# Streaming encoder step: silu of the conditioning columns ahead of the other loads, five gathered rows moved behind pass two's latents and nine placed in the gap before its routing, tile 0's end cut in three parts in the dense loop

## The chip, the cores and the metric

The kernel runs on one core of one Trainium2 chip, in Bass: each engine has its own instruction stream, and the streams meet only in semaphores. The metric is the device time of one execution in microseconds, the median of several runs.

## The reference, cut to what matters

One trunk layer for two request groups that share their weights: a prompt of 512 tokens and a sample of 32 tokens with 128 cached ones, model width 2048, all in fp32.

```python
mod = silu(c) @ w_ada + b_ada                 # shift1, scale1, gate1, shift2, scale2, gate2
h = rms_norm(x) * (1 + scale1) + shift1
proj = h @ w_in                               # queries, latents, keys, values, forget logits, two gates
lat = rms_norm(ckv);  k_nope, v = lat_all @ w_ukv
o_mla = chunk-causal softmax attention;  o_fox = causal attention with forget cumsums
merged = sigmoid(g_mla) * (o_mla @ w_o_mla) + sigmoid(g_fox) * (o_fox @ w_o_fox)
x = x + gate1 * (merged @ w_out)
h2 = rms_norm(x) * (1 + scale2) + shift2
q = h2 @ w_q                                  # 8 heads; top 16 of 128 + 128 keys, then top 16 of 256 sums
a = gelu(h2 . u_tab[expert]) * softmax(score) # 128 experts of 16384 for each token
x = x + gate2 * sum(a * v_tab[expert])
y = rms_norm(x) * final_g                     # the outputs are y and the new cache entries
```

## The kernel before

**Tiles and passes.** The 544 tokens are five tiles of up to 128: tiles 0 and 1 are group 0 (pass one), tiles 2 and 3 and the 32 sample tokens are group 1 (pass two). Both passes run the same stages: `mixers` (latents, eight heads of MLA, eight of FoX), `merge`, the output projection (`add_out`), the second norm and the query scores, from which VectorE picks the experts (`route`).

**Weights.** SP streams blocks of 1 MB from `wstream` into a ring of four slots, in the order of the list `SEQ`; a block is asked for when its slot has been used (line 389). The first 32 blocks make `mod`: 24 are multiplied on TensorE (`ada_row`, four rows and then a batch of columns, `ada_cols`), eight on VectorE (`mod_block`). TensorE's rows need the silu of `cT` (lines 807 and 808), VectorE's blocks the silu of `c_rows` (lines 809 and 810). ACT issues the loads of both, of `b_ada`, of the constants and of x_t (lines 800 to 806) ahead of both activations. After them it copies each ada row out of PSUM (`copy_rows`, line 831); TensorE's column batches wait for those copies, VectorE adds the bias to each batch (`rows_out`, line 1276), and between batches it squares x (`squares`, line 1270), for which it waits for x_t.

**The expert part.** A row is 1 MB: one row of `peer_u` or `peer_v` for each of 128 tokens, gathered by POOL (`gather_row`) into a slot; there are four slots in `first`, and four more, the ring's, once the dense loop has read its last block (the wait on `a_ps`, line 1884). VectorE takes the rows in the order of the list `ORDER`: 256 dot products (tiles 0 and 1), then 258 additions for the same tiles (two of them the residual rows), then 288 additions in 36 batches for tiles 2, 3 and the sample. The first 514 are the generator `shallow`; `take(n)` takes n of them wherever VectorE's program has room: in pass two's `mixers` as `fill`, in its merge, its output projection and its routing. What is left after the routing runs in `rest`, which does other steps at given row numbers: `N_GATES` (normalise the gates, then 26 steps of the sort by expert, one every two rows), `N_VAR0` and `N_SCALE0` (tile 0's final norm), `N_LAST` and `N_NEED` (how far the dense loop must be for each batch).

**The dense loop.** For tiles 2, 3 and the sample TensorE computes the product of every expert's `u` with every token: 128 blocks in 32 trips of four, with two PSUM banks (`dense`, line 754). ACT takes the gelu of each block and stores it to DRAM (`dense_out`, line 1153), from where POOL gathers the wanted values. TensorE leaves the loop at trip 14 (`T_RANKED`) for two transposes, for which it waits for the sort (`sort_ok`, line 770), and at trip 16 (`T_LAST`) for one, for which it waits for `last_ok`. ACT leaves it at trips 7 (`T_GATES`), 9 (`T_FIN0`) and 15 (`T_STORE0`). At trip 9 it does tile 0's `finish` (line 1165): wait for the residual, squares with a sum, then wait for VectorE's variance (`finish_var`, `y_rs`), root. At trip 15 it stores tile 0's output.

**In pass two's latents** VectorE takes 14 rows, then computes the latents' norm and the forget gates (`latents`, line 1323, one row inside), then takes eight rows, then rotates the first head's query. TensorE transposes the normed latents as they come (`lat_ok`, line 499). After the second norm VectorE waits for the first query unit, clears a part of the score buffer (line 1772), waits for the first scores and routes.

Of the kernel before, what the change touches and what calls it, by code (L numbers as in the profile page):

```python
# [6 lines left out]
D, TP, TS, PAST = 2048, 512, 32, 128  # L7
# [8 lines left out]
CG = (0, 2 * P, T)  # L16
# [124 lines left out]
def rows(t):  # L141
    return P if t < QT else TS
# [12 lines left out]
def build(nc, wstream, x_t, c_t, c_rows, b_ada, g1, g2, kvg, final_g, fbias, lat_cache, kr_cache, kf_cache, vf_cache,  # L155
          logf_cache, keys, peer_u, peer_v, aug_ones, consts, outs):
    F32, U32 = mybir.dt.float32, mybir.dt.uint32
    ACT, ALU, AX = mybir.ActivationFunctionType, mybir.AluOpType, mybir.AxisListType
# [8 lines left out]
    with ExitStack() as ctx:  # L167
# [187 lines left out]
        def unit_done(key):  # L355
            return UNIT[key] + 1
# [9 lines left out]
        S_COL = QT * SLOTS  # L366
        T_GATES, T_FIN0, T_RANKED, T_STORE0, T_LAST = 7, 9, 14, 15, 16
        BATCHES = ([(r, t) for r in range(R_ALT) for t in (2, 3)] + [(r, 2) for r in range(R_ALT, TOPK)]
# [5 lines left out]
        TAIL = len(ORDER) - FB * len(BATCHES)  # L374
        N_GATES, N_VAR0, N_SCALE0, N_LAST, N_NEED = 432, 452, 470, 500, TAIL - 1
        SORT_STEPS = 26
# [419 lines left out]
        def _(act):  # L796
            def a(out, in_, fn=ACT.Copy, **kw):
                return nc.scalar.activation(out, in_, fn, **kw)  # L798

            act.dma_start(cT[:, :, :], c_t).then_inc(c_in, 16)  # L800
            act.dma_start(late[:, 0:2 * D], c_rows.to_broadcast([P, 2 * D])).then_inc(crow_in, 16)
            act.dma_start(bad[:, :], b_ada).then_inc(bada_in, 16)
            act.dma_start(cst[:, :], consts).then_inc(cst_in, 16)
            for i in range(4):
                for g in range(2):
                    act.dma_start(og[g][:, 4 * i:4 * i + 4, :], x_t[:, 4 * i:4 * i + 4, CG[g]:CG[g + 1]]).then_inc(x_in[i], 16)
            act.wait_ge(c_in, 16)
            a(cT[:, :, :], cT[:, :, :], ACT.Silu).then_inc(silu_ok, 1)
            act.wait_ge(crow_in, 16)
            a(late[:, 0:2 * D], late[:, 0:2 * D], ACT.Silu).then_inc(crow_ok, 1)  # L810

# [352 lines left out]
            dense_out(0, True)  # L1164
            def finish(n, t, y):
                m = rows(t)
                act.wait_ge(y_pre, n + 1)
                a(sq_junk[0:m, :], y[0:m, :], ACT.Square, accum_out=stat[0:m, 0, t:t + 1])
                act.drain().then_inc(y_ss, 1)
                act.wait_ge(y_rs, n + 1)  # L1170
                a(stat[0:m, 1, t:t + 1], stat[0:m, 1, t:t + 1], ACT.Sqrt).then_inc(y_rs2, 1)

            def store(n, t, y):
# [12 lines left out]
            act.wait_ge(route_ok, 2)  # L1186
            finish(0, 0, h2_acc[0])
            with act.Fori(T_FIN0, T_STORE0) as i:
                dense_out(i)
# [24 lines left out]
        def _(dve):  # L1214
# [183 lines left out]
            def mixers(g, fill):  # L1398
                fill(14)
                latents(g, fill)  # L1400
                if g == 0:
                    dve.wait_ge(crow_ok, 1)
                fill(8)
                for i in range(NH):
# [47 lines left out]
            def second_norm(g):  # L1452
                dve.drain().then_inc(sq_ok, 1)
                norm(2 + g, [(pb[4], CG[g], CG[g + 1])])
                if g == 0:
                    coefs(g2T, 4 * KC)
                scaled(1 + g, (g,))
# [283 lines left out]
            def take(n):  # L1741
                for _ in range(n):
                    next(peer)
# [23 lines left out]
            for j in range(KC):  # L1767
                add_out(1, j)
                take(2)
            second_norm(1)  # L1770
            dve.wait_ge(proj, unit_done((1, "wq", 0)))
            v.memset(routing[1].s_head[:, :, 2, :, :], 0.0)
            dve.drain().then_inc(s_clear, 1)
            route(1, take)
            take(4)
# [264 lines left out]
```

## Time and profile before

| | us |
|---|---|
| median of 3 runs | 4278.77 (4278.7 to 4281.38) |
| the profiled execution | 4321.2 |
| its span, first to last instruction | 4319.4 |
| TensorE matmul busy | 3502.0 (81%) |
| VectorE busy | 2839.2 (66%) |
| GpSimd busy | 1461.3 (34%) |
| ACT busy | 388.0 (9%) |

Times in the rows are microseconds from the start of the span, unless marked ns. PE is TensorE's matmul, PEld its weight load, DVE is VectorE, ACT is ScalarE, POOL is GpSimd, SP is SyncE; a q behind the name is that engine's queue or sequencer. L401 is line 401 of the kernel; a line can be that of a helper, so L401 stands for every matmul and L798 for every activation.

### The profile page before, as it was taken

How to read it: one execution, taken by the hardware profiler on the slowest of the kernel's cores; microseconds unless marked ns; L12 is line 12 of the kernel's file. 1: busy time of each engine (PE TensorE's matmuls, PEld its weight loads, DVE VectorE, ACT ScalarE, POOL GpSimd, SP SyncE). 2: the span in 40 equal slices, each digit the busy share in tenths (PEclk: the TensorE clock that was granted, in tenths of full speed). 3: DMA queues.
4: the chain of work that ended last, by engine and by line, in shares of the span. 5: the costliest groups of instructions: out<-in, count | busy, mean ns of one | idle time of the engine just before them, and what ended most of it. 6: DMA issues, size and time to landing. Idle time of an engine off the chain costs nothing.

```text
span 4319.4 us, 39399 instructions
## 1 busy us (share of the span) xinstructions
PE 3502.0 (81%) x14249; PEld 2505.6 (58%) x14249; DVE 2839.2 (66%) x3456; ACT 388.0 (9%) x958; POOL 1461.3 (34%) x1094
## 2 busy tenths in 40 slices
PE   7899999999989999999986989997599998970000
PEld 5465678887845546467765667775476766750000
DVE  5354432237777886776677868986875566557998
ACT  0311110000212111010000011001000000000000
POOL 0000000000024544553343413233533666656764
PEclk9999999999999999989998999999799999995555
DMA  8577555557368998999999957789899999988997
GB/s 331 193 278 275 208 197 191 194 219 287 136 242 332 389 392 351 391 366 392 419 408 416 400 221 308 294 341 420 350 407 379 384 410 409 382 316 353 396 383 320
DMA packets 251314, 1412.71 MB, mean 327 GB/s; under 512 B 35312, under 2 KB 83456, under 8 KB 86144
## 3 DMA queue, kind: packets, MB, share of 16 engines
q0 software_dynamic: 124704, 841.18, 48.3%
q1 hardware_dynamic: 68832, 501.25, 30.0%
q10 hardware_dynamic: 57632, 68.41, 4.5%
q8 instruction: 84, 1.38, 0.1%
q14 instruction: 62, 0.51, 0.0%
HBM read 1359.60 MB, written 51.16 MB: 327 GB/s over the span
## 4 chain that ended last, share of the span: by engine, by line
PE 53%; DVE 17%; DMA 13%; issue 5%; POOL 2%; another core or an unknown queue 2%; PEld 2%; DVEq 2%; ACT 1%; ACTq 1%; PEldq 1%; SPq 0%
PE pq L401 52%; DMA first<-peer_v,experts 8%; DVE pq L1693 7%; DMA first<-peer_u,experts 4%; DVE late L1693 3%; POOL first L1849 2%; PEld pq L401 2%; DMA ring<-wstream 1%; DVE first L1683 1%; PE pq L405 1%; ACT arena L798 1%; DVE arena L1466 1%; DVE arena L1473 1%; DVE arena L1467 1%
## 5 line engine op out<-in xcount | busy, mean ns | idle before, releaser
L401 PE MATMUL pq<-h_last,ring 128*128 128x288 f32 (+2 forms) x6688 | 1712.3, 415 | 169.1 <-issue 78.1
L401 PEld LDWEIGHTS pq<-h_last,ring 128*128 128x128 f32 (+2 forms) x6688 | 1262.0, 191 | 612.3 <-issue 164.0
L1849 POOL DMA_INDIRECT first<-peer_u,experts x256 | 433.3, 1693 | 1731.8 <-DVEq L1528 1243.5
L1849 POOL DMA_INDIRECT first<-peer_v,experts x464 | 628.1, 1354 | 906.7 <-DVEq L1694 789.5
L1693 DVE SCALAR_TENSOR_TENSOR late<-first,wts,late 128x2048 f32<-128x2048 f32 x254 | 597.3, 2352 | 184.8 <-DMA first<-peer_v,experts 172.1
L401 PE MATMUL pq<-first,ring 128*128 128x256 f32 (+2 forms) x3104 | 702.1, 385 | 20.0 <-issue 9.0
L1683 DVE CUSTOM_DVE_ANT_0 first<-first,late 128x2048 f32<-128x2048 f32 x256 | 582.1, 2292 | 192.1 <-DMA first<-peer_u,experts 184.3
L401 PEld LDWEIGHTS pq<-first,ring 128*128 128x128 f32 (+2 forms) x3104 | 572.9, 187 | 143.1 <-issue 43.8
L1693 DVE SCALAR_TENSOR_TENSOR pq<-first,wts,pq 128x2048 f32<-128x2048 f32 x142 | 334.5, 2356 | 103.1 <-DMA first<-peer_v,experts 86.5
L1867 POOL DMA_INDIRECT got<-dots_dram,at_dot x288 | 317.0, 1101 | 126.7 <-issue 93.1
L401 PE MATMUL pq<-arena,ring 128*128 128x256 f32 (+2 forms) x1216 | 303.4, 407 | 46.0 <-DVEq L1435 32.1
L798 ACT ACTIVATE arena<-pq 128x256 f32<-128x256 f32 (+12 forms) x419 | 157.4, 402 | 1715.3 <-PE pq L401 1429.8
L401 PEld LDWEIGHTS pq<-arena,ring 128*128 128x128 f32 x1216 | 231.6, 194 | 116.9 <-issue 60.1
L1693 DVE SCALAR_TENSOR_TENSOR arena<-first,wts,arena 128x2048 f32<-128x2048 f32 x63 | 148.2, 2352 | 109.0 <-DMA first<-peer_v,experts 105.9
L1693 DVE SCALAR_TENSOR_TENSOR pq<-ring,wts,pq 128x2048 f32<-128x2048 f32 x80 | 188.4, 2355 | 36.8 <-DMA ring<-peer_v,experts 25.7
L401 PE MATMUL pq<-arena,cst 128*32 128x512 f32 x8 | 5.1, 795 | 251.0 <-issue 251.0
L1230 DVE CUSTOM_DVE_ANT_0 late<-ring,late 128x2048 f32<-128x2048 f32 x72 | 164.8, 2289 | 65.0 <-ACT late L798 29.4
L1431 DVE TENSOR_TENSOR arena<-arena,pq 128x256 f32<-128x256 f32 (+1 forms) x32 | 14.0, 437 | 268.6 <-ACTq L1083 267.6
L401 PE MATMUL pq<-arena 128*128 128x256 f32 (+12 forms) x592 | 153.2, 384 | 19.6 <-ACT arena L798 18.7
L1232 DVE CUSTOM_DVE_ANT_0 ring<-ring,late 128x2048 f32<-128x2048 f32 x72 | 164.6, 2287 | 0.0
L401 PEld LDWEIGHTS pq<-arena,cst 128*32 128x32 f32 x8 | 1.0, 144 | 254.3 <-issue 254.3
L401 PE MATMUL pq<-ring,h_last 128*128 128x512 f32 (+1 forms) x288 | 140.5, 619 | 2.9 <-issue 2.9
(197 smaller groups left out, 2002.2 us busy)
## 6 DMA issues: line engine op xcount, KB each, us to landing
ring<-wstream SPq DMA_DIRECT2D x478, 1024.0 KB
dots_dram<-wts ACTq DMA_DIRECT2D x8, 2304.0 KB, 8.4
dots_dram<-stage ACTq DMA_DIRECT2D x128, 144.0 KB
first<-peer_v,experts POOLq DMA_INDIRECT x464
got<-dots_dram,at_dot POOLq DMA_INDIRECT x288
first<-peer_u,experts POOLq DMA_INDIRECT x256
out<-arena ACTq DMA_DIRECT2D x6, 512.0 KB, 8.2
o_last<-x_t ACTq DMA_DIRECT2D x5, 576.0 KB, 11.1
```

The lines of the kernel that those rows point to most:

```text
L401: return nc.tensor.matmul(out, lhsT, rhs, start=start, stop=stop)
L405: return nc.tensor.transpose(out, in_, ident[0:p, 0:p])
L798: return nc.scalar.activation(out, in_, fn, **kw)
L1230: v.tensor_tensor_reduce(out=g2b, in0=ring[:, sl, :], in1=crow[:, 0, :], scale=1.0, scalar=0.0, op0=ALU.mult, op1=ALU.add, accum_out=msum[ ...
L1232: v.tensor_tensor_reduce(out=ring[:, sl, :], in0=ring[:, sl, :], in1=crow[:, 1, :], scale=1.0, scalar=0.0, op0=ALU.mult, op1=ALU.add, accu ...
L1466: v.max_index(ind[q][:, 0:8], val[q][:, 0:8], src[q])
L1467: v.match_replace(rest[q], val[q][:, 0:8], src[q], -3.0e38)
L1473: v.max_index(ind[q][:, 8:16], val[q][:, 8:16], rest[q])
L1683: v.tensor_tensor_reduce(out=row, in0=row, in1=h2, scale=1.0, scalar=0.0, op0=ALU.mult, op1=ALU.add, accum_out=wts[:, col:col + 1]).then_i ...
L1693: v.scalar_tensor_tensor(acc, row, w, acc, ALU.mult, ALU.add)
L1849: g.indirect_dma_start(out=slots[slot], out_offset=None, in_=peer_u if kind == "u" else peer_v, in_offset=bass.IndirectOffsetOnAxis(ap=exp ...
L1867: g.indirect_dma_start(out=got[:, i % LAPS, e:e + 1], out_offset=None, in_=dots_dram.rearrange("e (t o) -> (e t) o", o=1), in_offset=bass. ...
```

## The change

It has four parts. ACT waits for `cT` and takes its silu right after issuing the loads of `cT` and `c_rows`; then it issues `b_ada`, the constants and the first quarter of x_t, takes the silu of `c_rows`, and issues the other three quarters. In pass two VectorE takes nine rows ahead of the latents and thirteen behind them, instead of 14 and eight (in pass one these calls take none). Behind pass two's second norm it takes three rows before the wait for the first query unit and six before the routing; the marks in `rest` are renumbered. In the dense loop ACT does tile 0's squares at trip 9, its root at trip 13 (`T_ROOT0`), in a loop of its own from there, and its store at trip 15 as before.

```diff
--- before.py
+++ after.py
@@ -364,7 +364,7 @@
         NU = len(UNIT)
         TRIPS = NK // 4
         S_COL = QT * SLOTS
-        T_GATES, T_FIN0, T_RANKED, T_STORE0, T_LAST = 7, 9, 14, 15, 16
+        T_GATES, T_FIN0, T_ROOT0, T_RANKED, T_STORE0, T_LAST = 7, 9, 13, 14, 15, 16
         BATCHES = ([(r, t) for r in range(R_ALT) for t in (2, 3)] + [(r, 2) for r in range(R_ALT, TOPK)]
                    + [(r, QT) for r in range(QS // FB)] + [(r, 3) for r in range(R_ALT, TOPK)])
         ORDER = ([("u", 0, c) for c in range(SLOTS)] + [("u", 1, c) for c in range(SLOTS)]
@@ -372,7 +372,7 @@
                  + [("v", 1, c) for c in range(SLOTS)] + [("x", 1, 0)]
                  + [("v", t, FB * r + e) for r, t in BATCHES for e in range(FB)])
         TAIL = len(ORDER) - FB * len(BATCHES)
-        N_GATES, N_VAR0, N_SCALE0, N_LAST, N_NEED = 432, 452, 470, 500, TAIL - 1
+        N_GATES, N_VAR0, N_SCALE0, N_LAST, N_NEED = 438, 458, 480, 502, TAIL - 1
         SORT_STEPS = 26
         uses = [0] * (GR + RING)
         N_WIDE = TAIL + 2 * FB * R_ALT
@@ -799,15 +799,17 @@
 
             act.dma_start(cT[:, :, :], c_t).then_inc(c_in, 16)
             act.dma_start(late[:, 0:2 * D], c_rows.to_broadcast([P, 2 * D])).then_inc(crow_in, 16)
+            act.wait_ge(c_in, 16)
+            a(cT[:, :, :], cT[:, :, :], ACT.Silu).then_inc(silu_ok, 1)
             act.dma_start(bad[:, :], b_ada).then_inc(bada_in, 16)
             act.dma_start(cst[:, :], consts).then_inc(cst_in, 16)
-            for i in range(4):
+            for g in range(2):
+                act.dma_start(og[g][:, 0:4, :], x_t[:, 0:4, CG[g]:CG[g + 1]]).then_inc(x_in[0], 16)
+            act.wait_ge(crow_in, 16)
+            a(late[:, 0:2 * D], late[:, 0:2 * D], ACT.Silu).then_inc(crow_ok, 1)
+            for i in range(1, 4):
                 for g in range(2):
                     act.dma_start(og[g][:, 4 * i:4 * i + 4, :], x_t[:, 4 * i:4 * i + 4, CG[g]:CG[g + 1]]).then_inc(x_in[i], 16)
-            act.wait_ge(c_in, 16)
-            a(cT[:, :, :], cT[:, :, :], ACT.Silu).then_inc(silu_ok, 1)
-            act.wait_ge(crow_in, 16)
-            a(late[:, 0:2 * D], late[:, 0:2 * D], ACT.Silu).then_inc(crow_ok, 1)
 
             def root(n, c0, c1):
 
@@ -1162,13 +1164,20 @@
             act.wait_ge(zero_out, 16 * NH)
             gelu(1, SLOTS, SLOTS)
             dense_out(0, True)
-            def finish(n, t, y):
+            def finish_squares(n, t, y):
                 m = rows(t)
                 act.wait_ge(y_pre, n + 1)
                 a(sq_junk[0:m, :], y[0:m, :], ACT.Square, accum_out=stat[0:m, 0, t:t + 1])
                 act.drain().then_inc(y_ss, 1)
+
+            def finish_root(n, t):
+                m = rows(t)
                 act.wait_ge(y_rs, n + 1)
                 a(stat[0:m, 1, t:t + 1], stat[0:m, 1, t:t + 1], ACT.Sqrt).then_inc(y_rs2, 1)
+
+            def finish(n, t, y):
+                finish_squares(n, t, y)
+                finish_root(n, t)
 
             def store(n, t, y):
                 act.wait_ge(y_ok, n + 1)
@@ -1184,8 +1193,11 @@
                 dense_out(i)
             act.wait_ge(rt_used, 2 * PH)
             act.wait_ge(route_ok, 2)
-            finish(0, 0, h2_acc[0])
-            with act.Fori(T_FIN0, T_STORE0) as i:
+            finish_squares(0, 0, h2_acc[0])
+            with act.Fori(T_FIN0, T_ROOT0) as i:
+                dense_out(i)
+            finish_root(0, 0)
+            with act.Fori(T_ROOT0, T_STORE0) as i:
                 dense_out(i)
             store(0, 0, h2_acc[0])
             with act.Fori(T_STORE0, TRIPS) as i:
@@ -1396,11 +1408,11 @@
                 dve.drain().then_inc(prob_ok, 1)
 
             def mixers(g, fill):
-                fill(14)
+                fill(9)
                 latents(g, fill)
                 if g == 0:
                     dve.wait_ge(crow_ok, 1)
-                fill(8)
+                fill(13)
                 for i in range(NH):
                     if g == 0:
                         for q in range(2):
@@ -1768,9 +1780,11 @@
                 add_out(1, j)
                 take(2)
             second_norm(1)
+            take(3)
             dve.wait_ge(proj, unit_done((1, "wq", 0)))
             v.memset(routing[1].s_head[:, :, 2, :, :], 0.0)
             dve.drain().then_inc(s_clear, 1)
+            take(6)
             route(1, take)
             take(4)
             ranking = sort_by_expert()
```

## Rows read from the trace of the kernel before

**Rows 1.** The page, chain of work that ended last, by engine.

```profile
PE 53%; DVE 17%; DMA 13%; issue 5%; POOL 2%; another core or an unknown queue 2%; PEld 2%; DVEq 2%; ACT 1%; ACTq 1%; PEldq 1%; SPq 0%
```

**Rows 2.** Timeline, start: from, for, engine, line, operation, out<-in, count [idle before <-releaser].

```profile
0.76 0.41 ACTq L800 DMA_DIRECT2D cT<-c_t  x1
...
4.12 11.81 ACTq L806 DMA_DIRECT2D first<-x_t  x1
...
25.77 1.28 ACT L798 ACT_TABLE_LOAD   x1 [25.77 <-issue]
...
27.35 17.71 PE L401 MATMUL pq<-ring,cT 128*2 128x128 f32 x128 [27.35 <-ACT cT L798]
...
62.81 0.17 DVE L1221 TENSOR_TENSOR mod<-pq,bad 128x8 f32<-128x8 f32 x1 [6.41 <-PE pq L401]
```

**Rows 3.** DMA issues of the whole span: tiles, count, KB each, median us to landing.

```profile
late<-c_rows ACTq DMA_DIRECT2D x1, 2048.0 KB, 12.2
...
o_last<-x_t ACTq DMA_DIRECT2D x1, 1728.0 KB, 38.0
...
cT<-c_t ACTq DMA_DIRECT2D x1, 16.0 KB, 5.2
```

**Rows 4.** Transfers of the first 60 us; a full 5 us (last columns DMA share, GB/s).

```profile
DMA packets 6552, 20.58 MB, mean 343 GB/s; under 512 B 639, under 2 KB 4735, under 8 KB 4735
...
40.00:45.00 5.00, 4.89 (x44) 3.42 (x42) 0.77 (x1) 0.27 (x1) 0.00 (x0) 1.00 1.01 421
```

**Rows 5.** Timeline at pass two's latents; last, line 1683 alone in one stretch.

```profile
1276.02 2.29 DVE L1683 CUSTOM_DVE_ANT_0 first<-first,late 128x2048 f32<-128x2048 f32 x1 [0.81 <-DMA first<-peer_u,experts]
...
1292.80 2.29 DVE L1683 CUSTOM_DVE_ANT_0 first<-first,late 128x2048 f32<-128x2048 f32 x1 [0.18 <-DMA first<-peer_u,experts]
...
1298.87 2.53 PE L405 MATMUL pq<-cst,arena 128*128 128x128 f32 x12 [17.54 <-DVE arena L1346]
...
1344.00 0.45 DVE L1317 TENSOR_TENSOR arena<-arena,cst 64x288 f32<-64x288 f32 x1 [15.40 <-ACTq L961]
...
1305.00:1329.00 24.00, 18.14 (x16) 1.00 0.84 290
```

**Rows 6.** Timeline behind pass two's second norm: POOL's last gather before it, VectorE.

```profile
2526.62 0.94 POOL L1849 DMA_INDIRECT first<-peer_v,experts  x1 [2.98 <-DVEq L1694]
...
2546.18 1.34 DVE L1772 MEMSET arena<- 128x1536 f32 x1 [8.39 <-PE pq L401]
2565.18 1.26 DVE L1463 MAX8 arena<-arena 128x8 f32<-128x128 f32 x6 [17.67 <-ACTq L1103]
```

**Rows 7.** Timeline of the dense loop at trip 9, ACT and TensorE.

```profile
3065.74 0.20 ACT L798 ACTIVATE stat<-stat 128x1 f32<-128x1 f32 x1 [73.44 <-DVEq L1703]
...
3068.03 2.29 PE L401 MATMUL pq<-h_last,ring 128*128 128x288 f32 x4 [63.32 <-ACT stage L798]
```

**Rows 8.** Line 1693 by stretch (DVE busy, count, PEclk, DMA share, GB/s); timeline.

```profile
2918.00:2988.00 70.00, 42.92 (x19) 1.00 1.02 424
...
3068.00:3152.00 84.00, 50.79 (x22) 0.98 0.99 401
...
3153.74 8.02 PE L401 MATMUL pq<-h_last,ring 128*128 128x288 f32 x32 [0.71 <-issue]
...
3181.62 0.19 DVE L1647 SCALAR_TENSOR_TENSOR at_dot<-arena,cst 128x32 uint32<-128x32 f32 x1
...
3187.36 8.02 PE L401 MATMUL pq<-h_last,ring 128*128 128x288 f32 x32 [0.71 <-issue]
...
3220.78 0.41 PE L405 MATMUL pq<-cst,arena 128*128 128x128 f32 x2 [0.49 <-issue]
```

**Rows 9.** Timeline behind the dense loop: POOL, ACT, VectorE.

```profile
3858.86 0.94 POOL L1849 DMA_INDIRECT ring<-peer_v,experts  x1 [25.86 <-PE pq L401]
...
3961.14 2.06 ACT L798 ACTIVATE o_last<-pq 128x512 f32<-128x512 f32 x4 [81.31 <-remote]
...
3965.36 0.15 DVE L1700 TENSOR_SCALAR stat<-stat 128x1 f32<-128x1 f32 x1 [24.21 <-ACTq L1169]
```

## The prediction

> **What bounds the kernel now.** I read the chain of work that ended last first: it runs through TensorE for half of the span, then through VectorE and the row gathers [rows 1]. A share over the whole span says little here, since TensorE alone ends the first two thirds and the rows the last third, so I went on stage by stage: the timeline of the start, of pass two's latents, of the gap behind pass two's second norm, of the dense loop at trip 9, and of the end.
>
> At the start TensorE stands until 27.35 us. It needs the silu of cT (16 KB, landed 5.2 us after an issue at 0.76 us) and gets it only when ACT has issued all eight loads of x_t; the third of these held ACT's queue for 11.81 us [rows 2, 3]. In pass two TensorE stands 17.54 us before the latents' transposes, because VectorE is still in the last of 14 rows taken ahead of them; later VectorE stands 15.40 us, having taken its eight rows behind them [rows 5]. Behind the second norm VectorE stands 8.39 us and, after one memset, 17.67 us more [rows 6]. In the dense loop ACT stands 73.44 us in tile 0's finish, waiting for VectorE's variance, and TensorE, with both banks full, 63.32 us [rows 7]. That chain is what sets the end: the gather of row 647 waits until the dense loop's last block is done (line 1884), and had waited 25.86 us for it [rows 9]. From there on the tail is a fixed number of rows. So the end moves with the end of the dense loop, as long as the rows reach their gate before it.
>
> The profiled execution (4321.2 us, span 4319.4) lies 1.0% above the median of the timed runs. I make the sum on its rows and take it off the median.
>
> **Columns' silu first.** It moves one wait and one activation ahead of ten issues, and the rows' silu ahead of six. The value for TensorE: cT lands at 0.76 + 5.2 = 6.0 us; the table load and the activation took 27.35 - 25.77 = 1.58 us before [rows 2], so TensorE can start between 6.3 us (table loaded during the wait) and 7.6 us; I take 7, a start 20.3 us earlier. That is the upper end. It can't all be kept, because the transfers are then late. By 60 us 20.58 MB had moved, in the 421 GB/s that a full stretch shows this takes 48.9 us, and I allow 2 us for the first transfers to get going: the same state of loads is there 60 - 51 = 9 us earlier and no more [rows 4]. The DMAs that move on ACT's queue: b_ada and the constants go out about 5 us later, still before TensorE has four rows done (17.71 us after its start); six loads of x_t go out behind the rows' silu, which waits for c_rows (12.2 us to landing) [rows 2, 3]. Queued behind these issues on ACT are the copies of the ada rows (line 840), without which TensorE stops after its fourth row. In the trace loads of x_t gave way to other traffic: 1728 KB took 38.0 us once [rows 3]; ACT may so be held issuing until about 32 us, when the fourth row's copy would come at 33 us against 45 before, which leaves 10 to 14. VectorE's second batch of columns, at 62.81 us before, is then at 49 to 55 us. If x_t lands much later than that, VectorE's squares hold the batches and only some 4 us are left. I take 11 us, with 4 and 20 as ends. From the second batch on the stage goes at TensorE's pace as before, and all that follows waits for it, so the gain goes through.
>
> On that point the Trainium skill ("DMA: Bandwidth & Descriptors", Queues, rings and completion order) says that each DMA engine goes round its queues packet by packet, a packet holding several descriptors. By that rule the two queues share about evenly and the gain would be 8 us rather than 11; the 38.0 us of 1728 KB in [rows 3] show a smaller share for x_t than even, so I keep 11.
>
> **Nine rows ahead of the latents instead of fourteen.** Row 9 ends at 1276.02 + 2.29 = 1278.3 us, row 14 at 1295.1 [rows 5]. Freed at 1278.3, VectorE then waits for ACT's rope copies; TensorE's previous work, which needs the same copies, ended at 1298.87 - 17.54 = 1281.3, so they are there at about 1281.0. From VectorE's start to the first transpose took 1298.87 - 1295.1 = 3.8 us, so the transposes come at 1284.8: 14.1 us earlier. ACT's square root and table loads come in this stretch too and may cost 1 to 4 us more: ends 10 and 14.5. The five rows go behind: thirteen instead of eight, from about 1291.4 us. Eight rows (16 instructions) lie in 24 us of that place, 3.0 us each [rows 5]; thirteen end near 1331, and the next step, 1344.00 before, is due at 1329.9. One or two us late there are hidden, since TensorE projects keys at that time. If the cover failed wholly, the price would be 5 x 3.0 = 15 us and the gain nothing. I take 14.
>
> **Nine rows in the gap.** Three go into the 8.39 us, six into the 17.67 us [rows 6]; VectorE needs 50.79 / 22 = 2.3 us for one [rows 8], 6.9 and 13.9 us. Queued behind them on VectorE are the memset that frees ACT's first query copies, and the routing. The four slots had been asked for by 2526.62, 11 us before the gap, and the other five come at 3.0 us apiece once the first is free at about 2540: the last near 2562, before 2565.18. So they cost nothing; if they came at the dense loop's 3.7 us, the routing would start 3 us late. What they give: every mark in the later rows is reached nine rows, 9 x 3.7 = 33 us, earlier relative to the dense loop. That alone moves no end, but the next part needs it.
>
> **Tile 0's end in three parts.** The squares stay at trip 9, the root goes to trip 13, the store stays at trip 15. TensorE's 63.32 us go [rows 7], since the variance (row 458) is then done some two trips before it is asked for, as the next lines give it. What is late next is trip 14, where TensorE waits for the sort (line 770). Counted without the shift of the two earlier parts: trip 9's first two blocks end at 3068.03 - 63.32 = 3004.7 [rows 7]; a trip takes 3187.36 - 3153.74 = 33.6 us [rows 8], so it starts at 2988 and trip 14 is due at 3156. The sort's 26 steps run over 50 rows, from row 440, which falls where row 431 fell before: row 413 ended at 2918, and 19 rows lie from there to 2988 [rows 8], so at about 2987. Row 458 then comes at 2987 + 18 x 3.7 = 3054, trip 13 at 3122. Rows beside the full dense loop took 70 / 19 = 3.68 us each, with sort steps between them 84 / 22 = 3.82 [rows 8], while the transfers were at 401 to 424 GB/s: 184 to 191 us, so the sort is ready at 3171 to 3178, and some 5 us less since the last rows go faster while TensorE stands. Before it was ready at 3181.8 and asked for at 3220.78, without a wait [rows 8]. So TensorE waits 10 to 22 us there anew; I take 17, with ends 0 (rows at 3.4) and 40 (rows at 4.2 in the heavy steps). Trip 16 asks for the last experts at row 502, twelve rows on, 46 us against two trips of 67: covered. Net of this part 63.3 - 17 = 46 us, ends 23 and 63. Rows then reach their gate 34 us earlier and the dense loop ends 46 us earlier, and as the rows were early by 25.86 [rows 9], they are still there first. The renumbered marks and the root's table loads (1.3 us at most, [rows 2], where ACT otherwise waits for TensorE) cost nothing.
>
> **Sum.** 11 + 14 + 46 = 71 us: 4278.8 - 71 = **4208 us**.
>
> **Rivals.** *The sort keeps what the finish gave.* If the rows are slower beside a dense loop that no longer stands, TensorE waits 40 us at trip 14 instead of 17 and the start gives only its low end: 4 + 14 + 23 = 41 us, 4238. For it: the transfers are full there [rows 8]; against: 50 rows would need 4.2 us each.
> *The wait at the end goes or moves out.* After its last loop ACT stood 81.31 us released by nothing that the profile names, and VectorE 24.21 us behind it [rows 9]. Other code ahead of that place may remove it: 4208 - 24 = 4184. Against: nothing in the change aims at it.
> *Slower.* ACT's loop is cut once more inside the dense loop. If a hold like that of 81.31 us came at a new cut, TensorE's two banks would cover two blocks, 16.8 us, and it would lose 64.5: with one hold 4272, no difference to be seen; with holds at both ends of the two new trips 4208 + 129 = 4337, slower. It decides from the second hold on. Against: no boundary of the loops at trips 7, 9 and 15 shows one; TensorE came to trip 14 with 0.49 us of idle time [rows 8].
> The Trainium skill ("Runtime: NRT & Kernel Launch", Instruction fetch mechanics) has the rule behind such a hold: a taken branch whose target is outside the two pages at hand must fetch by DMA first. No run here shows that this was the cause of the 81.31 us.
>
> **How the numbers follow.** Forecast 0.66 (own range 4188 to 4230), sort 0.12, end wait gone 0.13, one hold 0.06, two holds 0.03. The range leaves out the holds and the far ends of the bounds: 4168 to 4246. A measurement of this kernel can tell about 0.2%, 8.6 us, from no change: faster 0.92, same 0.05, slower 0.03.
>
> **What would show it.** TensorE's first matmul at 6 to 8 us and pass two's first latents 20 to 30 us earlier; TensorE's idle time before the latents' transposes under 5 us; nine rows between the second norm and the routing, which starts no later relative to it; no wait of ACT for line 1703 in the dense loop, and one of TensorE ahead of the first transposes of line 405 in it, 10 to 25 us; the dense loop's end some 70 us earlier and the rows' gate still waiting for it. The prediction is wrong if the start's gain is gone by pass one, if the wait at trip 14 is over 40 us, or if the rows come to their gate after the dense loop's end.

## The result, and the profile after

The changed kernel took 4244.72 us (4242.57 to 4246.88, four runs) against 4279.88 us: a ratio of 0.9918, interval 0.9900 to 0.9935, that is 35 us less (28 to 43). Measured once more beside its parts it had a ratio of 0.9895 (0.9873 to 0.9917), 45 us less (36 to 54). Two single executions, one of the kernel before (7604 us) and one of the finish alone (14420 us), are left out of every figure below. The forecast was 71 us less, 4208; the time lies inside the range, near its upper end. About half of the expected gain is missing.

The profiled execution took 4246.88 us, span 4244.5. That is 75 us under the profiled execution of before, twice what the timed runs give: about 40 us of the difference are a matter of that one execution of before, which the first experiment shows.

The page's chain of work that ended last, by engine, of the changed kernel (before: [rows 1]):

```profile
PE 48%; DMA 17%; DVE 17%; POOL 6%; issue 6%; DVEq 2%; PEld 2%; ACT 1%; PEldq 1%; ACTq 1%; POOLq 0%; SPq 0%
```

These shares differ too much between executions to be compared: in second profiles they are PE 52%, DMA 15%, POOL 6% for the kernel before and PE 35%, DMA 22%, POOL 11% for the changed one. Nor has the dense loop left the chain. In this execution it is followed until a block that ends at 3770.87, and then over the store of its values to POOL's gather of the dots (chain that ended last, in order of time):

```profile
3762.86 8.01 PE pq L401 x32
...
3771.47 4.20 DMA dots_dram<-stage
3775.67 2.17 POOL got L1881
```

POOL's idle time ahead of that gather is 0.30 us, as between most of its gathers: here loop and rows are level. The start in the timeline, which answers to [rows 2]:

```profile
5.97 0.23 ACT L798 ACTIVATE cT<-cT 128x32 f32<-128x32 f32 x1 [3.00 <-DMA cT<-c_t]
6.25 5.71 PE L401 MATMUL pq<-ring,cT 128*2 128x128 f32 x32 [6.25 <-ACT cT L798]
13.15 3.66 PE L401 MATMUL pq<-ring,cT 128*2 128x128 f32 x32 [1.18 <-DMA ring<-wstream]
15.70 12.56 ACTq L812 DMA_DIRECT2D o_last<-x_t  x1
20.98 8.95 PE L401 MATMUL pq<-ring,cT 128*2 128x128 f32 x64 [4.18 <-DMA ring<-wstream]
28.86 7.86 ACTq L812 DMA_DIRECT2D o_last<-x_t  x1
39.73 0.74 ACT L798 ACTIVATE mrow<-pq 2x128 f32<-2x128 f32 x4 [22.81 <-issue]
40.57 1.84 PE L401 MATMUL pq<-cst,mrow 2*128 2x2 f32 x8 [10.64 <-ACT mrow L798]
61.50 0.17 DVE L1233 TENSOR_TENSOR mod<-pq,bad 128x8 f32<-128x8 f32 x1 [8.15 <-PE pq L401]
```

TensorE begins at 6.25 us, as forecast, but then waits for weight blocks, and after its fourth row 10.64 us for ACT's copies, which stood behind two loads of x_t that held ACT 12.56 and 7.86 us. The second batch of columns comes at 61.50 instead of 62.81. The first matmul of pass one's latents comes at 142.33 instead of 145.02: 2.7 us of the forecast 11. In the six executions with the old start that matmul comes at 143.81 to 146.82, in the six with this new one at 141.39 to 143.85.

Pass two's latents, the gap, and the dense loop at trips 13 and 14 (to [rows 5 to 8]), still from the timeline:

```profile
1285.42 2.53 PE L405 MATMUL pq<-cst,arena 128*128 128x128 f32 x12 [2.90 <-DVE arena L1358]
...
2546.44 1.34 DVE L1785 MEMSET arena<- 128x1536 f32 x1 [1.19 <-PE pq L401]
...
2564.90 2.35 DVE L1705 SCALAR_TENSOR_TENSOR late<-first,wts,late 128x2048 f32<-128x2048 f32 x1 [2.88 <-DMA first<-peer_v,experts]
...
3124.82 0.20 ACT L798 ACTIVATE stat<-stat 128x1 f32<-128x1 f32 x1
...
3180.52 0.69 PE L405 MATMUL pq<-cst,arena 128*128 128x128 f32 x2 [24.48 <-DVEq L1661]
```

The wait ahead of the transposes is 2.90 us instead of 17.54; the nine rows fit into the gap; the root at trip 13 waits for nothing; TensorE waits 24.48 us at trip 14 where 17 was forecast. And yet the memset behind the second norm comes at the same time as before, 2546.44 against 2546.18.

The end, last block of the dense loop and first gather into the ring (to [rows 9]):

```profile
3779.48 8.00 PE L401 MATMUL pq<-h_last,ring 128*128 128x288 f32 x32 [0.26 <-issue]
...
3808.10 0.94 POOL L1863 DMA_INDIRECT ring<-peer_v,experts  x1 [0.30 <-issue]
```

The loop ends at 3787.5, and POOL comes to its gate 20.6 us later, without a wait. The prediction named just this as what would prove it wrong: the rows come after the loop's end.

### The profile page after: what moved, and what is told of

The parts are those of the page before. It is cut to its first block, busy times and chain, and to the rows that moved or that the text cites. A ratio compares the mean times of both kernels' runs of the same rounds, so it can differ in the third digit from the quotient of the medians.

```text
span 4244.5 us, 39396 instructions
## 1 busy us (share of the span) xinstructions
PE 3510.5 (83%) x14249; PEld 2510.1 (59%) x14249; DVE 2838.9 (67%) x3456; ACT 382.1 (9%) x954; POOL 1483.6 (35%) x1094
## 4 chain that ended last, share of the span: by engine, by line
PE 48%; DMA 17%; DVE 17%; POOL 6%; issue 6%; DVEq 2%; PEld 2%; ACT 1%; PEldq 1%; ACTq 1%; POOLq 0%; SPq 0%
PE pq L401 47%; DMA first<-peer_v,experts 10%; DMA first<-peer_u,experts 6%; DVE pq L1705 5%; POOL first L1863 4%; DVE late L1705 3%; PEld pq L401 2%; DVE first L1695 2%; POOL got L1881 2%; DMA ring<-wstream 2%; PE pq L405 1%; ACT arena L798 1%; POOL ring L1863 1%; ACTq L812 1%; DVE arena L1478 1%
## 5 line engine op out<-in xcount | busy, mean ns | idle before, releaser
L1863 POOL DMA_INDIRECT first<-peer_u,experts x256 | 419.7, 1639 | 1746.2 <-DVEq L1540 1243.4
L1863 POOL DMA_INDIRECT first<-peer_v,experts x464 | 660.7, 1424 | 843.5 <-DVEq L1706 752.2
L1242 DVE CUSTOM_DVE_ANT_0 late<-ring,late 128x2048 f32<-128x2048 f32 x72 | 164.8, 2289 | 50.7 <-DMA ring<-wstream 24.5
## 6 DMA issues: line engine op xcount, KB each, us to landing
first<-peer_u,experts POOLq DMA_INDIRECT x256, 10.1
```

What stands on the lines that cost most here:

```text
L1242: v.tensor_tensor_reduce(out=g2b, in0=ring[:, sl, :], in1=crow[:, 0, :], scale=1.0, scalar=0.0, op0=ALU.mult, op1=ALU.add, accum_out=msum[ ...
L1863: g.indirect_dma_start(out=slots[slot], out_offset=None, in_=peer_u if kind == "u" else peer_v, in_offset=bass.IndirectOffsetOnAxis(ap=exp ...
```

## The experiments

Two theories were set against each other. **R**: the rows and their transfers set the end, the dense loop's end doesn't. **D**, the prediction's own: the dense loop's end sets it.

### Before, a second time

> The kernel before, unchanged, profiled a second time. Theory (the profiled execution of before had a slow end that the timed runs don't have): its time is 4278 to 4285 us, ACT's 81 us wait behind the dense loop and VectorE's 24 us behind it are gone or under 10 us, and the rows between 3800 and 4000 us run at a transfer share near 1.00 instead of 0.79 and 0.88; the dense loop may still end near 3855 or earlier. Rival (the excess is typical of a profiled run of before): about 4320 us again, with the 81 us wait at the same place.

It took 4284.48 us, beside 4286.8 as the median of before on that chip. Timeline of that execution:

```profile
3822.78 8.00 PE L401 MATMUL pq<-h_last,ring 128*128 128x288 f32 x32 [0.26 <-issue]
...
3845.12 0.95 POOL L1849 DMA_INDIRECT ring<-peer_v,experts  x1 [0.30 <-issue]
...
3927.99 0.20 ACT L798 ACTIVATE stat<-stat 128x1 f32<-128x1 f32 x1 [73.26 <-DVEq L1703]
```

The dense loop ends at 3830.8 (3858.6 in the first execution), POOL reaches its gate 14.3 us after that and doesn't wait. The 25.86 us of [rows 9], on which the prediction hung the end, and the 81.31 us of ACT with them, belong to one execution. The copy out of PSUM that had waited 81.31 us waits 5.58 us here; the 73.26 us above are another wait, that of tile 1's `finish` for VectorE's variance. Between 3800 and 3900 and between 3900 and 4000 us the transfers' share is 0.93 and 1.02 instead of 0.79 and 0.88. The stall at trip 9 is the same (63.73 us). So already before the change the rows were late at the gate, and the theory on the excess holds.

### The parts alone

The silu alone, on before:

```diff
+            act.wait_ge(c_in, 16)
+            a(cT[:, :, :], cT[:, :, :], ACT.Silu).then_inc(silu_ok, 1)
             act.dma_start(bad[:, :], b_ada).then_inc(bada_in, 16)
...
-            act.wait_ge(c_in, 16)
-            a(cT[:, :, :], cT[:, :, :], ACT.Silu).then_inc(silu_ok, 1)
```

> Before plus the first part alone (silu of the columns first, x_t's quarters split around the silu of the rows). Theory (the start's gain is spent by x_t's loads and by the clock, and what is left is lost where the rows wait for transfers): first latents matmul 2 to 4 us earlier than 145.02, second norm's memset within 2 us of 2546, time -3 to +2 us. Rival (the start's gain goes through): -7 us or more.

Ratio 0.9998 (0.9982 to 1.0014): 1 us less, between 8 less and 6 more, as the theory had it. First latents matmul at 142.40; pass two's transposes at 1301.15, where the five executions with the old start and the old latents have 1298.9 to 1302.9.

The latents alone:

```diff
-                fill(14)
+                fill(9)
                 latents(g, fill)
...
-                fill(8)
+                fill(13)
```

> Before plus the second part alone (nine rows ahead of pass two's latents, thirteen behind). Theory (transfers bind pass two from 1300 us on, so the rows come when the transfers allow): TensorE 13 us earlier at head 1, 0 to 3 us earlier at the second norm's memset (2546), time -4 to +1 us. Rival (TensorE binds and the gain was lost to stretches of its clock at 1.2 GHz that differ from execution to execution): 8 to 13 us earlier at the memset in an execution with as many such stretches as before, time -6 to -13 us.

Ratio 0.9978 (0.9962 to 0.9995): 9 us less (2 to 16), inside the rival's band. The transposes come at 1283.40, the memset at 2529.54, some 20 us earlier than in the second execution of before. My theory, that transfers take the 13 us back, falls: they go through. Why the changed kernel showed nothing of them at its memset is answered below.

The gap alone, the finish alone, and both:

```diff
             second_norm(1)
+            take(3)
...
+            take(6)
             route(1, take)
```

```diff
-            finish(0, 0, h2_acc[0])
-            with act.Fori(T_FIN0, T_STORE0) as i:
+            finish_squares(0, 0, h2_acc[0])
+            with act.Fori(T_FIN0, T_ROOT0) as i:
+                dense_out(i)
+            finish_root(0, 0)
+            with act.Fori(T_ROOT0, T_STORE0) as i:
                 dense_out(i)
```

> Before plus the third part alone: nine rows in the gap with the renumbered marks; tile 0's finish stays whole at trip 9. Theory R (the rows and their transfers set the end; in an ordinary execution of before POOL's first gather into the ring comes 14 us after the dense loop's end): the rows come 20 to 25 us earlier, the stall of TensorE at trip 9 stays at 55 to 70 us because the variance is now asked of row 458, the dense loop's end stays, and the gate then takes effect: time -13 to -22 us. Rival D (the dense loop's end sets the end, as the prediction had it): time 0 to -5 us.

> Before plus the fourth part alone: tile 0's end in three parts, marks and gap as before. Theory R: TensorE waits 22 to 28 us at trip 14 instead of 64 at trip 9, the dense loop ends 35 to 42 us earlier, but the rows come only 5 to 13 us earlier and so does the end: time -5 to -13 us. Rival D: time -25 to -40 us.

> Before plus the third and fourth part together (nine rows in the gap with the renumbered marks, and tile 0's end in three parts); start and latents as before. Theory (the whole gain is here: 9.9 MB more moved in the gap, worth 25 us at 400 MB per ms, and 5 MB more at trip 9, worth 13 us): time -31 to -38 us, as the whole change. Rival (the early parts carry a third of the gain): -15 to -25 us.

The gap alone: ratio 0.9981 (0.9963 to 0.9998), 8 us less (1 to 16). The finish alone: 0.9978 (0.9960 to 0.9996), 9 us less (2 to 17). Both: 0.9924 (0.9895 to 0.9953), 33 us less (20 to 45), in the band of its theory. The gap's 8 us lie between its bands: R asked for 13 to 22, D for 0 to 5. The timeline of the finish alone:

```profile
3199.90 0.69 PE L405 MATMUL pq<-cst,arena 128*128 128x128 f32 x2 [36.47 <-DVEq L1659]
...
3798.58 8.00 PE L401 MATMUL pq<-h_last,ring 128*128 128x288 f32 x32 [0.26 <-issue]
...
3849.82 0.94 POOL L1859 DMA_INDIRECT ring<-peer_v,experts  x1 [0.30 <-issue]
```

This is the run that decides. The last block, begun at 3798.58, ends near 3806.6, 24 us earlier than in the second execution of before, and the first gather into the ring comes 4.7 us later than there: the loop's end moved and the rows didn't follow. D asked for 25 to 40 us less; 9 came, inside R's 5 to 13. R's marks on the way were missed, though: TensorE waits 36.47 us at trip 14 instead of 22 to 28, the loop ends 24 us earlier instead of 35 to 42, and the rows, said to come 5 to 13 us earlier, came no earlier in this execution. Where the 9 us of the time come from is therefore not shown.

All traces agree on the main point. From the first gather into the ring to the end of the span it is 436.4 to 437.8 us in thirteen of the fourteen executions (460.5 in the first of before), and in those thirteen that gather comes 4.3 to 43.2 us behind the loop's end. So the end follows that gather, and the gather doesn't wait for the loop's end. And the gap alone:

```profile
3073.84 10.57 PE L401 MATMUL pq<-h_last,ring 128*128 128x288 f32 x32 [62.37 <-ACT stage L798]
...
3295.30 0.28 DVE L1658 TENSOR_REDUCE last_f<-pq 2x16 f32<-2x128 f32 x1 [13.97 <-PE pq L405]
```

The rows run some 25 us ahead up to row 502; there VectorE wants the last experts' transpose, which TensorE, late by its stall at trip 9, does at trip 16, and stands 13.97 us; POOL, whose first gather of dots needs what VectorE computes from it, stands 31.08 us there, and 12.4 to 16.0 us in the other executions. So the gap alone is held by the stall that the finish removes; with both edits the 13.97 us are gone. Against the second execution of before the stretch from pass two's memset to the end is 11.0 us shorter with the gap, 1.1 us longer with the finish and 32.6 us shorter with both. The times alone (8 and 9 against 33) leave open, by their intervals, whether the pair gives more than the sum.

### The sort begun earlier

```diff
-        N_GATES, N_VAR0, N_SCALE0, N_LAST, N_NEED = 438, 458, 480, 502, TAIL - 1
+        N_GATES, N_VAR0, N_SCALE0, N_LAST, N_NEED = 426, 458, 480, 502, TAIL - 1
```

> The changed kernel with the sort begun at row 426 instead of 438 (one mark; every other mark as it is). Theory R (rows and transfers set the end, the dense loop's end doesn't): TensorE's wait of 24 to 27 us at trip 14 falls under 3 us, the dense loop ends 20 to 26 us earlier, and the end stays: time -4 to +4 us against the changed kernel. Rival D (the dense loop's end sets the end): 15 to 25 us below the changed kernel.

Ratio 0.9881 (0.9861 to 0.9900), against 0.9895 (0.9873 to 0.9917) for the changed kernel on another chip: 6 us less, with overlapping intervals. The wait at trip 14 is gone (6.13 us at trip 16 in its place), the loop ends at 3763.1, 24 us earlier than in the changed kernel. D's 15 to 25 us didn't come. But R's "the end stays", within 4 us, isn't met cleanly either: from the memset to the end this execution is 10 to 15 us shorter than the two of the changed kernel. What of the loop's end reaches the rows is left open at that size.

### The changed kernel again

> The changed kernel, unchanged, profiled and timed again beside its parts. Theory (the latents' 13 us are real, and in the first profile of the changed kernel they were lost to longer stretches of the clock at 1.2 GHz between 1300 and 2000 us, which differ from execution to execution): time -36 to -48 us, 5 to 12 us below the third and fourth part alone; memset behind the second norm between 2528 and 2550 us, earlier the shorter those stretches are. Rival (rows or start take the 13 us back in this kernel every time): memset at 2544 to 2549 again, time -29 to -36 us, no better than the third and fourth part alone.

45 us less (36 to 54), as the theory had it; but the memset came at 2545.02, inside both bands (2528 to 2550 and 2544 to 2549): that row decides nothing.

### The start with the copies first

```diff
-            for i in range(1, 4):
-                for g in range(2):
-                    act.dma_start(og[g][:, 4 * i:4 * i + 4, :], x_t[:, 4 * i:4 * i + 4, CG[g]:CG[g + 1]]).then_inc(x_in[i], 16)
+            load_x(1)
...
-            for i in range(4):
+            rows_trip(0)
+            load_x(2)
+            load_x(3)
+            for i in range(1, 4):
                 rows_trip(i)
```

> The changed kernel with the last two quarters of x_t issued by ACT behind its copies of the first four ada rows, instead of ahead of them. Theory (ACT, held 12.6 and 7.9 us in issues of x_t, made TensorE's columns wait 10.6 us and used up most of what the silu gave): the copies follow the fourth ada row within 2 us, TensorE's wait ahead of the first batch of columns falls under 2 us, the second batch comes at 50 to 56 us instead of 61.5, the first latents matmul at 133 to 138 us instead of 142. Rival (the transfers bind the start; VectorE's squares of x_t's late quarters hold the second batch): second batch at 59 us or later, first latents matmul at 140 us or later. Time: by the first 2 to 10 us below the changed kernel, by the rival within 3 us of it; a measurement of this kernel hardly tells these apart, the trace does.

The start of its timeline:

```profile
30.53 1.02 PE L401 MATMUL pq<-cst,mrow 2*128 2x2 f32 x8 [0.40 <-ACT mrow L798]
31.48 14.94 PE L401 MATMUL pq<-ring,cT 128*2 128x128 f32 x128
...
43.32 1.22 DVE L1292 TENSOR_TENSOR first<-first 128x1024 f32<-128x1024 f32 x1 [2.98 <-DMA o_last<-x_t]
...
55.68 0.17 DVE L1239 TENSOR_TENSOR mod<-pq,bad 128x8 f32<-128x8 f32 x1
...
57.80 12.47 PE L401 MATMUL pq<-ring,cT 128*2 128x128 f32 x87 [9.96 <-DMA ring<-wstream]
```

The hold of ACT was real: without it the wait ahead of the columns goes from 10.64 to 0.40 us, and the second batch comes at 55.68 as forecast. But the next wait takes its place: TensorE stands 9.96 us for a weight block, and the first latents matmul comes at 139.94, 2.4 us earlier than in the changed kernel, not 4 to 9. In the last run below, which has the same edit, it comes at 142.40, no earlier than in the changed kernel. The theory holds for the copies, the rival for the stage. The ratio is 0.9886 (0.9865 to 0.9906), 49 us less than before and 4 less than the changed kernel on another chip, which its interval doesn't tell from nothing.

### The hole behind the routing heads

```diff
                     dve.drain().then_inc(rt_used, 1)
+                    fill(3)
...
-                    fill(7)
+                    fill(4)
```

> The changed kernel with the seven rows behind each routing head of pass two split: three behind the head's first selection, four at its end. VectorE idled 28.5 us for the gathers behind the heads, while the transfers stood at a share of 0.77. Theory R (filling a hole of the transfers brings the rows and the end forward by as much): the idle time falls to under 8 us, the routing ends 18 to 28 us earlier, the transfers' share there rises to 0.82 or more, time 15 to 28 us below the changed kernel. Rival (the rows beside the dense loop are bound by transfers whatever comes ahead of them, or the gate of the dense loop takes over at once): under 8 us below the changed kernel.

Groups by line, VectorE, from the gap to the end of the routing: first the changed kernel, then this one (busy, mean, idle before and its releaser).

```profile
L1705 DVE SCALAR_TENSOR_TENSOR late<-first,wts,late 128x2048 f32<-128x2048 f32 x55 | 129.4, 2353 | 33.6 <-DMA first<-peer_v,experts 29.5
```

```profile
L1706 DVE SCALAR_TENSOR_TENSOR late<-first,wts,late 128x2048 f32<-128x2048 f32 x52 | 122.3, 2351 | 8.9 <-issue 2.3 <-DMA first<-peer_v,experts 2.0
```

Idle time for gathers falls from 29.5 to 2.0 us, the transfers' share between 2546 and 2868 us rises from 0.77 to 0.83, the last head ends at 2868.5 instead of 2891.5, and the ratio to before is 0.9831 (0.9806 to 0.9857): 73 us less. That is 27 less than the changed kernel on the same chip by the ratios, 21 by the medians (4224.09 against 4245.49); R forecast 15 to 28.

> The changed kernel with eight rows in two parts of four at each routing head of pass two, instead of seven at its end (the kernel with three and four had 23 us over the changed one). Theory R: the seven rows more cost 2.35 us of VectorE each in a stage where the transfers stand at 0.80 to 0.90, and save 3.7 us each beside the dense loop: 5 to 12 us below three and four, that is 28 to 36 us below the changed kernel. Rival (the transfers of the stage are now full, or the gate of the dense loop takes over): within 4 us of three and four, or slower.

> Eight rows in two parts at each routing head, and the last two quarters of x_t issued behind the first copies of ada rows: the two edits together on the changed kernel. Theory: the sum of both, 30 to 45 us below the changed kernel. Rival: as the one with the rows alone, 28 to 36 us below it, since the start's gain is lost ahead of pass two.

With four and four rows the ratio is 0.9842 (0.9819 to 0.9865), no better than with three and four: the rival holds. VectorE now reaches row 480 12.44 us before tile 0's root at trip 13 is done: the marks weren't moved along. With the copies first as well it is 0.9823 (0.9800 to 0.9846), 76 us less; that lies in the bands of both theories, and the times don't tell whether the start's edit gave anything. The three lie within each other's intervals, and all beat both kernels.

## Where the time went: three accounts

From the windows by stretch (DMA share, PE busy, granted clock) one account can be made for each stage. They are accounts, not causes: they say in which resource a saving must show.

**From the memset to the end.** I summed, in windows of 50 us up to 20 us before the end, (1 - DMA share) x length, shares over 1 taken as 1:

| kernel | memset to end | transfers idle | time less idle and the last 20 us |
|---|---|---|---|
| before, the profile of the start | 1773.2 | 171.2 | 1582.0 |
| before, second profile | 1732.1 | 134.6 | 1577.5 |
| silu / latents | 1734.3 / 1730.2 | 135.5 / 132.8 | 1578.8 / 1577.4 |
| gap / finish | 1721.1 / 1733.2 | 124.1 / 131.9 | 1577.0 / 1581.3 |
| gap and finish | 1699.5 | 108.2 | 1571.3 |
| changed, two profiles | 1698.1 / 1702.9 | 106.8 / 106.1 | 1571.3 / 1576.8 |
| sort early | 1688.0 | 103.4 | 1564.6 |
| rows_first | 1700.6 | 108.4 | 1572.2 |
| 3 + 4 / 4 + 4 / best | 1683.6 / 1684.5 / 1677.8 | 85.4 / 88.8 / 83.2 | 1578.2 / 1575.7 / 1574.6 |

All move 636 MB in 1565 to 1582 us of transfers; the rest is holes. The change is worth 29 to 34 us here, of which 28 are holes filled. Two of them, in windows of before's second execution and then of the changed kernel (the last two columns are DMA share and GB/s):

```profile
2500.00:2600.00 100.00, 85.62 (x335) 60.44 (x334) 63.36 (x133) 18.72 (x49) 20.85 (x10) 0.93 0.56 212
3000.00:3100.00 100.00, 34.78 (x132) 25.56 (x130) 87.05 (x69) 3.35 (x7) 50.96 (x28) 0.68 0.87 340
```

```profile
2500.00:2600.00 100.00, 85.55 (x334) 60.36 (x333) 82.26 (x138) 18.71 (x49) 37.43 (x20) 0.93 0.78 303
3000.00:3100.00 100.00, 95.22 (x382) 71.38 (x381) 84.29 (x63) 4.92 (x12) 45.61 (x27) 1.00 1.01 418
```

The gap's rows fill 22 us of transfers ((0.78 - 0.56) x 100), the split finish 13 (0.87 to full); at trip 14's new wait the share falls to 0.94. The profiled execution of before has 36.6 us more of holes than its second profile: that is its excess over the median.

One stretch ahead of the gate has another limit. In the changed kernel POOL has no pause over 0.30 us from 3775 to 3808 us, with up to two gathers of dots between two rows, while the transfers stand for much of it (the same columns):

```profile
3780.00:3790.00 10.00, 9.41 (x47) 7.25 (x45) 4.42 (x3) 0.41 (x1) 8.17 (x7) 1.00 0.54 177
```

There POOL's own gathers set when the rows go out, and not the transfers; no run tries what that is worth.

**Pass two**, from the transposes to the memset, took 1242 to 1264 us in fourteen executions. Take TensorE's idle time off, and half of the time at the lower granted clock (1.2 GHz, at which eight column matmuls took 1.84 us instead of 1.02): 1063 to 1070 in all of them. The stage is TensorE's, and its length moves with the stretches at 1.2 GHz, 128 to 177 us, different in each execution: 151 in the first profile of before and 177 in that of the changed kernel, half of which is 13 us. By this account that, and not the rows, ate the 13 us in those two traces. Over all executions the transposes come at 1301.3 us with 14 rows ahead (mean of six) and at 1284.9 with nine (mean of eight, seven of them with the new start), the memset at 2553.2 and 2537.7.

**The start**, to the first latents matmul, took 139.9 to 146.8 us; less the holes of its transfers (20.5 to 25.8 us) it is 119.4 to 122.1 in all fourteen, whoever starts first.

## Why the prediction was right or wrong

- **Columns' silu, 11 forecast.** The step from "a start 20.3 us earlier" to "the same state of loads is there 9 us earlier" is the one that failed (and the 11 taken is more than the 9 which that step allowed). By 60 us the kernel before had moved 20.58 MB [rows 4] and the changed kernel hardly more; the difference of 0.35 MB is 0.8 us at 421 GB/s:

```profile
DMA packets 6596, 20.93 MB, mean 349 GB/s; under 512 B 640, under 2 KB 4736, under 8 KB 4736
```

  What stood in between first was ACT: the prediction had it issuing until about 32 us and the fourth row's copy at 33; it issued until 39.6, copied at 39.73, and the second batch came at 61.50 where 49 to 55 was forecast. The 38.0 us of 1728 KB [rows 3], which I used for that hold and against an even share, belong to a load that is issued at 2346.9 us, in pass two; the loads of x_t at the start took medians of 10.1 and 14.5 us to landing. Left were 2.7 us at the first latents, nothing by pass two's transposes, 1 us in the time (8 less to 6 more). My bound "4 if x_t holds the squares" was nearest by luck: ahead of the second batch VectorE waited 8.15 us for TensorE, not for x_t. The rule weighed there (the Trainium skill, "DMA: Bandwidth & Descriptors", Queues, rings and completion order: queues are served in turn, packet by packet) gave 8 us; the trace gives neither 8 nor 11, and no run separates the sharing between the queues from ACT's hold.
- **Nine rows ahead of the latents, 14 forecast.** Right: over all executions the transposes come 16 us earlier and the memset 15.5; alone the edit gave 9 us in the time (2 to 16). The forecast mark, 20 to 30 us at the latents, was too large by the start's part.
- **Nine rows in the gap, 0 by themselves.** They cost little: the last of them ends 20.8 us behind the start of the memset, where the routing began 19.0 us behind it before. But alone they gave 8 us (1 to 16) where 0 was said, since the rows, not the loop, set the end.
- **Tile 0's end, 46 forecast.** Its mechanics were right: 63 us gone, a new wait at trip 14 of 24.5 and 26.6 us (10 to 22 forecast), the loop's end 43 us earlier than in the second execution of before. The step that failed is the first paragraph's "the end moves with the end of the dense loop". It rested on one wait of 25.86 us [rows 9] in an execution that was 1% over the median; the second execution has none: there the rows come 14.3 us behind the loop's end, so it was the rows' own gain that counted. The prediction had them 34 us earlier at the gate; they came 37.0 us earlier than in that execution (3845.12 and 3808.10), 33.0 counted from the memset. I had noted that 1% and taken the sum off the median, but had not asked which rows were in the excess. Finish and gap together gave 33 us instead of 46.
- **The sum** is then 0 to 3 + 9 to 16 + 33, some 42 to 52 us, against 35 and 45 measured. That 4245 us lies inside the range is owed to its width; two of the three terms were too large.
- **Rivals.** That the sort keeps the finish's gain, 4238, came nearest in time, though by another mechanism. No hold came at the two new cuts of ACT's loop: the root at 3124.82 follows its table load at once. The rule on branches that must fetch (the Trainium skill, "Runtime: NRT & Kernel Launch", Instruction fetch mechanics) thus has no row here that bears on it, and ACT's 81.31 us didn't come again.

## What to carry to other kernels

Before a sum rests on one wait, look whether the profiled execution is an ordinary one: an execution over the median has its excess somewhere, and it may be the wait on which the sum rests. Ask of each stage which resource can't lose time there (here transfers, then TensorE with its clock, then transfers again): an edit gives what it fills of that resource's holes, wherever it removes waits. Where one edit lifts the wait that holds the other's gain, cost them as a pair: from the memset to the end the traces give 11.0 and -1.1 us alone and 32.6 together.

## What the hardware showed that was not expected

- The issue of one x_t load held ACT's queue for 12.56 us, and with it 0.74 us of copies on which TensorE waited.
- Starting TensorE earlier cost it clock. In the first 120 us the granted clock was 1.2 GHz for 0 to 3.4 us in the kernels with the old start and for 13.6 to 20.6 us in those with the new one, in which TensorE began, stood and began again. Behind the 10.64 us for ACT's copies, in the changed kernel, four rows took 17.71 us; in the run with the copies first, without that wait, the same matmuls took 14.94 us. The kernel before pays this once too: its first four rows took 17.71 us [rows 2].

```profile
42.34 17.71 PE L401 MATMUL pq<-ring,cT 128*2 128x128 f32 x128
```

- Time at the lower clock in pass two differs by 49 us (128 to 177) between executions of kernels whose work there is alike, and is the main part of the spread of its length.
